# Up projections of a hybrid attention block as pairs of tiles with seven products each

## The reference, cut to what matters

```python
h = x @ w_in + b_in                       # x: 1024 x 1024, w_in: 1024 x 5376, float32
q_a, k_a, v_a, gate_a, q_b, k_b, v_b, gate_b, mg_a, mg_b = split(h)
o_a = swa_sink_attention(rope(q_a), rope(k_a), v_a, sinks) * silu(gate_a)   # 1024 x 512
y_a = o_a @ w_up_a                        # 512 x 1024
o_b = stick_breaking_attention(q_b, k_b, v_b) * silu(gate_b)                # 1024 x 512
y_b = o_b @ w_up_b                        # 512 x 1024
merged = sigmoid(mg_a) * y_a + sigmoid(mg_b) * y_b
out = layer_norm(ALPHA * x + merged @ w_out, ln_g, ln_b)
```

## Time and profile before

| what | us |
|---|---|
| median of three runs (lowest to highest) | 729.1 (729.04 to 729.34) |
| the profiled execution | 729.14 |
| its span, first to last instruction | 727.4 |
| TensorE busy | 716.8 |
| VectorE busy | 515.1 |
| ScalarE busy | 406.9 |
| GpSimd busy | 104.3 |

### The profile page before, as it was taken

How to read it: one execution, slowest core, us unless ns; L and a number is a source line. 1 busy time by engine, 2 the same in 40 slices (tenths; PEclk the granted TensorE clock), 3 DMA queues, 4 the chain that set the end, 5 groups by cost and what they waited for, 6 DMA issues and landing times.

```text
span 727.4 us, 10778 instructions
## 1 busy us (share of the span) xinstructions
PE 716.8 (99%) x4046; PEld 585.9 (81%) x4046; DVE 515.1 (71%) x736; ACT 406.9 (56%) x722; POOL 104.3 (14%) x130
## 2 busy tenths in 40 slices
PE   8999999999999999999999999999999999999996
PEld 7888877777888888888888888888888888888885
DVE  6998788756978988997798773665593556550644
ACT  6954477766766767776777764555581212240321
POOL 0000000000421322222223200000000000000782
PEclk9999999999999999999999999999999999999999
DMA  8236332231110201021021213455636343160451
GB/s 298 107 93 124 108 98 73 73 102 43 44 48 12 74 16 59 15 73 31 30 73 73 73 59 131 142 187 187 236 130 232 131 173 133 69 230 2 158 186 62
DMA packets 41491, 76.22 MB, mean 105 GB/s; under 512 B 12256, under 2 KB 16864, under 8 KB 41440
## 3 DMA queue, kind: packets, MB, share of 16 engines
q1 hardware_dynamic: 41440, 75.54, 31.7%
HBM read 55.07 MB, written 18.35 MB: 101 GB/s over the span
## 4 chain that ended last, share of the span: by engine, by line
PE 96%; DVE 2%; DMA 1%; issue 0%; ACT 0%; SPq 0%; POOL 0%; POOLq 0%; DVEq 0%; ACTq 0%
PE ps L222 26%; PE ps L224 26%; PE ps L223 26%; PE ps L1710 5%; PE ps L1722 5%; PE ps L1695 4%; PE ps L1639 1%; PE ps L1651 1%; PE ps L1620 1%; DMA xr<-in_xt 1%; DVE keep L1362 1%; PE ps L1674 0%; PE ps L1608 0%; DVE o_t L1525 0%; DVE o_t L1516 0%
## 5 line engine op out<-in xcount | busy, mean ns | idle before, releaser
L222 PE MATMUL ps<-x_hi,w_hi 128*128 128x512 f32 x416 | 167.3, 402 | 1.4 <-DVE x_lo L1269 1.4
L224 PE MATMUL ps<-x_hi,w_lo 128*128 128x512 f32 x416 | 162.6, 391 | 0.0
L223 PE MATMUL ps<-x_lo,w_hi 128*128 128x512 f32 x416 | 162.2, 390 | 0.0
L222 PE MATMUL ps<-t_ops,w_hi 128*128 128x512 f32 x304 | 121.4, 399 | 0.3 <-issue 0.3
L224 PE MATMUL ps<-t_ops,w_lo 128*128 128x512 f32 x304 | 118.7, 390 | 0.0
L223 PE MATMUL ps<-t_ops,w_hi 128*128 128x512 f32 x304 | 118.5, 390 | 0.0
L1212 DVE TENSOR_TENSOR w_lo<-raw,w_hi 128x512 fp32r<-128x512 f32 x120 | 81.6, 695 | 50.6 <-ACT w_hi L752 50.2
L1362 DVE TENSOR_TENSOR_SCAN keep<-keep 128x895 f32<-128x895 f32 (+4 forms) x64 | 86.4, 1380 | 15.5 <-POOL keep L697 15.5
L222 PEld LDWEIGHTS ps<-x_hi,w_hi 128*128 128x128 f32 x416 | 78.2, 188 | 17.7 <-issue 3.0
L224 PEld LDWEIGHTS ps<-x_hi,w_lo 128*128 128x128 f32 x416 | 78.1, 188 | 16.9
L223 PEld LDWEIGHTS ps<-x_lo,w_hi 128*128 128x128 f32 x416 | 78.3, 188 | 14.4
(11 more groups left out here) (189 smaller groups left out, 1118.8 us busy)
## 6 DMA issues: line engine op xcount, KB each, us to landing
raw<-in_w SPq DMA_DIRECT2D x28, 512.0 KB, 3.8
raw<-in_w SPq DMA_DIRECT2D x42, 256.0 KB, 2.7
sig_m<-sig_d SPq DMA_DIRECT2D x16, 512.0 KB, 4.2
sig_d<-sig_m SPq DMA_DIRECT2D x28, 256.0 KB, 3.8
xr<-in_xt SPq DMA_DIRECT2D x16, 256.0 KB, 6.0
raw<-in_xn SPq DMA_DIRECT2D x8, 512.0 KB, 3.7
out<-o_t SPq DMA_DIRECT2D x16, 256.0 KB, 2.2
o_t<-o_d SPq DMA_DIRECT2D x7, 512.0 KB, 4.9
```

What stands on the lines that cost most here:

```text
L222: pe.matmul(out, w_hi, x_hi, start=first, stop=False, skip_group_check=goes_on)
L223: pe.matmul(out, w_hi, x_lo, start=False, stop=False, skip_group_check=goes_on)
L224: return pe.matmul(out, w_lo, x_hi, start=False, stop=last, skip_group_check=goes_on)
```

## The change

The up projections are made as four more pairs (20 to 23, products 140 to 167), in the same loop as the input projection. A pair is two tiles of output features. For each branch apart, its 512-deep product is a 2 x 2 block problem with two depth tiles per block, and seven products do instead of eight. The two branches share a product number: the first half of product q (2 depth tiles x 3 matmuls) is branch A's, into bank 2(q%2), the second is branch B's, into the bank behind it. So a product has 12 matmuls as before, and ScalarE reads two banks, 1024 elements, at once.

- GpSimd makes the differences of the branches' quarters, four per branch (`up_sums`), after the fourth gate product. The last two, t = 4, wait until VectorE has split the quarter that they overwrite.
- ScalarE and VectorE split seven operands per branch, fourteen of 128x1024, at the products that `UP_SPLITS` names (133, 134, 136, 137, 139, 140, 142).
- Weights of the up pairs go through `load_a1`, `load_a2`, `weight_sums`, `part_high` and `low_part` as those of the input pairs.
- Merge gates come back per block of the pair (`up_gates`), and VectorE multiplies the finished block in SBUF by them and adds the two branches (`merge(j, b)`).
- The gates of branch A are made every four products (`GATE_A_AT`) and outputs come back earlier (`OUTPUTS_BACK`); the last output of branch B goes through DRAM too.
- The banks of the output projection are rotated by one pair.

```diff
+UP_PAIRS = KT // 2
+ALL_PAIRS = N_PAIRS + UP_PAIRS
+ALL_PRODUCTS = NP * ALL_PAIRS
+GATE_A_AT = (106, 110, 114, 118)
+OUTPUTS_BACK = (104, 105, 108, 111, 112, 114, 116, 118)
+UP_SPLITS = {LAST_PAIR: 0, LAST_PAIR + 1: 1, LAST_PAIR + 3: 2, LAST_PAIR + 4: 3, LAST_PAIR + 6: 4, LAST_PAIR + 7: 5,
+             LAST_PAIR + 9: 6}
+UP_BLOCKS = ((0, 0), (0, 1), (1, 1), (1, 0))
...
+            def up_sums(t, ab):
+                def quarter_of(kh, nh):
+                    return branch_part(kh, nh, ab)
+                o = up_sum(t, ab)
+                if t == 1:
+                    if ab == 0:
+                        pool.wait_ge(ga_set, GROUP)
+                    else:
+                        for k in range(GROUP, KT):
+                            pool.wait_ge(o_back[k], 16)
+                    pool.tensor_tensor(o, quarter_of(0, 1), quarter_of(0, 0), ALU.subtract).then_inc(u_raw[t], 1)
+                elif t == 2:
+                    pool.wait_ge(u_raw[1], ab + 1)
+                    pool.wait_ge(z_done, STEPS)
+                    pool.tensor_tensor(o, quarter_of(1, 1), up_sum(1, ab), ALU.subtract).then_inc(u_raw[t], 1)
+                elif t == 3:
+                    pool.wait_ge(u_raw[1], ab + 1)
+                    pool.tensor_tensor(o, quarter_of(1, 1), o, ALU.subtract).then_inc(u_raw[t], 1)
+                else:
+                    pool.wait_ge(u_raw[2], ab + 1)
+                    pool.wait_ge(ol_done, 2 + ab + 1)
+                    pool.tensor_tensor(o, o, up_sum(2, ab), ALU.subtract).then_inc(u_raw[t], 1)
             for s in range(STEPS):
                 cut_causal(s)
+            for t in range(1, 5):
+                for ab in range(2):
+                    up_sums(t, ab)
...
+            def branch_hi(pos, ab):
+                act.wait_ge(product_done, LAST_PAIR + pos + 1)
...
+                act.activation(up_operand(op_hi, pos, ab), up_source(pos, ab), ACT.Copy).then_inc(oh_done, 1)
...
+                if i >= N_PAIRS:
+                    j, b = i - N_PAIRS, pos // 2
...
+                    act.activation(up_other(pos) if pos % 2 else up_made(b), ps[:, 2 * (q % 2):2 * (q % 2) + 2, :],
+                                   ACT.Copy).then_inc(bank_read, 1)
...
+            def merge(j, b):
+                m, nh = UP_BLOCKS[b]
+                o, e = up_made(b), 4 * j + b
+                dve.wait_ge(sig_in[b], 16 * (j + 1))
...
+                dve.tensor_tensor(o, o, up_gate(b), ALU.mult).then_inc(up_mul, 1)
+                dve.wait_ge(up_mul, e + 1)
+                dve.wait_ge(ol_done, 10 if j == 0 else 2 * NP)
+                dve.tensor_tensor(o_t[:, 2 * j + m, half(nh)], o[:, 0, :], o[:, 1, :], ALU.add).then_inc(m_set, 1)
...
+                if q // NP == N_PAIRS:
+                    pe.wait_ge(ol_done, 2 * (q % NP) + part + 1)
...
+                    if q < N_PRODUCTS:
+                        last = mma3(pe, ps[:, q % 2, :], w_h[:, wk], w_l[:, wk], x_h[:, k, :], x_l[:, k, :],
+                                    k == 0 and not goes_on, k == 3, goes_on)
+                    else:
+                        last = mma3(pe, ps[:, 2 * (q % 2) + part, :], w_h[:, wk], w_l[:, wk], x_h[:, k, :],
+                                    x_l[:, k, :], k == 2 * part and not goes_on, k == 2 * part + 1, goes_on)
...
-            for j in range(KT):
-                up(j)
```

More of the change, by code:

```diff
@@ L67, in tile_of @@
     return PAIR_TILES + 2 * sp + m
-def up_tile(j):
-    return UP_0 + j
 def whole(n):
-    return n if n < PAIR_TILES else n - 2 * N_PAIRS
+    return n if n < PAIR_TILES else PAIR_TILES + n - W_OUT
 def raw_buffer(n):
-    return n if n < PAIR_TILES else (n - UP_0) % 4
+    return n if n < PAIR_TILES else (n - W_OUT) % 4
 def raw_loads(n):
-    return sum(raw_buffer(m) == raw_buffer(n) for m in (K_A, V_A, *range(UP_0, n + 1)) if m <= n)
+    return sum(raw_buffer(m) == raw_buffer(n) for m in (K_A, V_A, *range(W_OUT, n + 1)) if m <= n)
 def ring_half(n):
@@ L922, in split_next @@
                     part_high(n)
-                if pos == 3 and i - MG_PAIR - 3 in range(GROUP):
-                    gate_a_sigmoid(i - MG_PAIR - 3)
-                if i == N_PAIRS - 1 and pos < 4:
-                    for k in (2 * pos, 2 * pos + 1):
-                        branch_hi(k)
-                if q == N_PRODUCTS - 3:
-                    weight_hi(UP_0)
+                if q in GATE_A_AT:
+                    gate_a_sigmoid(GATE_A_AT.index(q))
+                if q in UP_SPLITS:
+                    for ab in range(2):
+                        branch_hi(UP_SPLITS[q], ab)
             for h in range(2):
@@ L1240, in after, with merges @@
                 rotations(q)
-                if q // NP == N_PAIRS - 1 and q % NP < 4:
-                    for k in (2 * (q % NP), 2 * (q % NP) + 1):
-                        branch_lo(k)
+                if q - 1 in GATE_A_AT:
+                    gate_a_product(GATE_A_AT.index(q - 1))
+                merges(q)
+                for ab in range(2):
+                    if q in UP_SPLITS:
+                        branch_lo(UP_SPLITS[q], ab)
+            def merges(q):
+                j, pos = q // NP - N_PAIRS, q % NP
+                if j >= 1 and pos in (0, 2):
+                    merge(j - 1, 2 if pos == 0 else 3)
+                if j >= 0 and pos in (3, 6):
+                    merge(j, 0 if pos == 3 else 1)
             def rotations(q):
@@ L1418, in _ @@
             gated_out(STEPS - 1)
-            for q in range(STEP_END + 2, N_PRODUCTS - 3):
+            for q in range(STEP_END + 2, ALL_PRODUCTS - 2):
                 after(q)
```

293 lines of the change are left out of this document (147 added, 146 removed).

## The result

The changed kernel takes 732.57 us (median of 5 runs, 732.19 to 733.37), the kernel before beside it 729.04 (728.99 to 729.34): a ratio of 1.0049, 95% interval 1.0037 to 1.0060. It is slower by 3.5 us, where 727.6 and a gain of 1.5 were forecast; the range ended at 732.2. One execution of run e6, at 2,726 us, stands apart from all others and is left out; it is also the only one of e6 that was traced.

The account below looks back on a forecast made before the run. TensorE, busy 99% of the span, was taken to bound the kernel. 729.14 - 10.9 (matmuls gone) + 3.8 (first stall) + 5.4 (second stall) + 0.1 (handover) = 727.6 us, range 719.8 to 732.2, own range 725 to 730.5.

Parts of the forecast that it names:

- What goes: Up stage on TensorE: 384 matmuls become 336, 48 fewer at 0.2267 us each, saving 10.9 us.
- The first stall: Product 127 waits about 3.8 us for its low part, behind VectorE instructions alternating with GpSimd's first six differences.
- a turn: One GpSimd difference and one VectorE instruction excluding each other for whole instructions: 2.2 + 0.55 us, reckoned as 2.74.
- The second stall: Products 142 and 143 wait for ScalarE's reads during the quarters' splits: 4.3 us, 5.4 in all.
- The two holds: GpSimd's last two differences blocking VectorE during the quarters' splits, 2.2 us each; without them the stall was 2.0 us.
- the walk: Step-by-step reckoning of VectorE's and ScalarE's queues from product 133 through the quarters' splits, giving 5.4 us.
- The handover: From last up product to output projection: low splits done at 10.8 us, needed at 10.9; 0.1 us added, loads nothing.
- The sum: Whole kernel: 729.14 - 10.9 + 3.8 + 5.4 + 0.1 = 727.6 us.
- 1 (weak exclusion): Long GpSimd instructions block VectorE weakly or not at all; only the 2.0 us burst remains: 720.3 us, chance 0.24.
- 2: Slower than before: full-length exclusion, hold 2.58, turns 3.27, stalls 6.9 and 6.5 us: 731.7 us, chance 0.19.
- 3: Everything added is hidden, no stall anywhere: 718.2 us, chance 0.05.
- 4: VectorE bounds the up pairs, 17.8 of 19.04 us: 0.3 to 1 us more per pair, 729 to 731, chance 0.06.

Follow-up runs that it names:

- e6: Changed kernel with SyncE issuing the first two output projection weight loads one product earlier in the last up pair: 730.39 us, ratio 1.0020.
- e8: Changed kernel with the edits of e5, e6 and e7 together: 720.51 us, ratio 0.9881 to the kernel before.
- e1: Changed kernel with GpSimd's eight differences replaced by fills with zeros, so up branches are computed from wrong sums: 722.06 us, ratio 0.9907.
- e3: Changed kernel with 36 idle transposes on TensorE ahead of product 127: 731.69 us, ratio 1.0033.
- e9: Changed kernel with e6's earlier loads, 36 idle transposes ahead of product 127 and 28 ahead of 142: 727.86 us, ratio 0.9987.
- e7: Changed kernel with the last three places of the up branch cuts moved one to two products later: 733.45 us, ratio 1.0054.
- e11: e8 with TensorE waiting ahead of product 127 for eleven short GpSimd fills of a spare tile: 725.94 us, ratio 0.9956.
- e2: Changed kernel with GpSimd's first six differences each held back to every second low part: 727.03 us, ratio 0.9972.
- e4: Changed kernel with each GpSimd difference of 1024 elements cut into two of 512: 732.6 us, ratio 1.0043.
- e5: Changed kernel with the eight differences made by VectorE instead of GpSimd, two of them at product 135: 724.62 us, ratio 0.9944.
- e10: e8 with TensorE waiting ahead of product 127 for six short GpSimd fills of a spare tile: 722.59 us, ratio 0.9914.
- e12: e8 with the up branch cuts after product 139 spread by branch: 719.74 us, ratio 0.9881.

## Why the prediction was wrong

- **What goes, 10.9 us:** right. The distances are 0.2268, and e8's sum closes to 0.01 with it.
- **The first stall, 3.8:** right in place, order and cause, 0.6 too small. A difference alone takes 2.40 (2.41 taken), but a turn is 2.81 instead of 2.74 and six stand ahead of low part 127, and the fourth gate product ends 2.7 us into product 121 instead of 2.4. The Trainium skill's rule for the two engines ("SBUF — State Buffer", "Who interferes with whom") has VectorE's two-input instructions contend with GpSimd's reads and not with its writes; both the 2.88 us rows and the fills of e1 that disturb nothing agree. The 4.5 us for 2048 elements of the Trainium skill's "GPSIMD Engine Reference", section 3.1, gave an estimate of 2.25; the trace has 2.40, and that stands.
- **The second stall, 5.4:** 5.24, right in cause. The two holds fell on a low part and a split, where the walk had two low parts. The walk also missed that product 140 waits too (0.87), for a read behind the first of the two sigmoids, and had the later ones that much too long.
- **The handover, 0.1, and loads "nothing":** the step that failed by its size, 1.91. I walked VectorE's low splits and not the issue of the load that ScalarE's high parts need: on SyncE it stands behind a wait for merges. The sentence that the loads land 1 us or more before use was not worked out from a row.
- **The sum:** the step that failed by its kind. It adds the stalls as waits only and lets TensorE go on at full speed after each; the 2.70 us of clock at the 1.2 GHz level aren't in it. With those, the 1.81 more at the handover, 0.63 at the first stall and 0.49 at 482.96, less 0.16 at the second, 727.6 becomes 733.0.
- **Rivals.** 1 (weak exclusion) fell by the 2.8 us rows. 2 came near in time (731.7) for a reason that doesn't hold: it wanted turns of 3.27 and a first stall of 6.9, and the trace has 2.81 and 4.43. 3 fell with both stalls. 4 fell: the steady pairs run without a wait at 17.8 of 19.04 us.
- Without the clock the changed kernel would stand at some 729.9, inside the forecast range and still no gain (e3's three executions without a drop took 730.07 to 731.14); the clock and the late loads decide the sign, as e9 shows, which has neither drops nor late loads: 727.86. What stays open is which waits bring the clock down: in the traces 4.43 (here), 4.26 (e7), 3.70 (e11), 3.36 (e2), 2.76 (e4) and 2.11 us (e2) did, 3.38 (e3, e4), 3.34 (here, at 142), 2.23 (e5) and 2.12 (e10) did not.

## What to carry to other kernels

Work given to an idle engine isn't free where it reads the memory that the busy vector engine reads: a difference of 2.40 us on GpSimd cost VectorE 2.2 us each time both had work, and made by VectorE itself it cost 1.22. Price a wait of the matmul engine of 2 us and more at itself and up to 2.7 us on top, and count late loads by where their issue stands in the queue, not by how long they take. Fewer matmuls pay in full only if the engines that feed them keep their lead; here three edits outside the matmuls took 732.6 to 720.5, and a fourth, the cuts spread by branch, to 719.7.

## What the runs showed of the hardware

- The granted clock fell to the 1.2 GHz level during or just after a wait of TensorE of 2.11 to 4.43 us; distances go from 0.227 to 0.427 us, and the price was 1.5 to 2.7 us. The runs of e2, e3, e4, e5, e7 and e11, with waits of 2.2 us and more, spread over 2.3 to 3.7 us, those of e8 and e10 over 0.4, and the longer executions mostly have the lower mean clocks. A long wait isn't the only way to a longer execution: single ones of e1 (723.45), e12 (722.29) and the kernel before (730.89) stand 1.2 to 2.4 us above the others of their kernel, at mean clocks of 0.996, 0.996 and 0.995, and none of them was traced.
- Idle transposes in the wait kept the clock: 1.00 through the first stall in the traces of e3 and e9.
- GpSimd's subtraction of two SBUF inputs takes 2.40 us for 1024 elements alone; a fill of as many takes 0.95 and leaves VectorE at 0.69. In turns, VectorE's 512 elements show 2.88 beside 1024 of GpSimd and 1.77 beside 512.
